# Splitting the first weight granule of five layer handovers into spare activation chunks, and giving the third granule's low part to POOL

## The reference, cut to what matters

```python
def swiglu(x, w_gate, w_up, w_down):
    return (jax.nn.silu(x @ w_gate) * (x @ w_up)) @ w_down
...
    for layer in range(DEPTH):
        f = swiglu(rmsnorm(h, nw[0]), ffn_w_gate[layer, 0], ffn_w_up[layer, 0], ffn_w_down[layer, 0])
        h = h + FFN_RES_SCALE * rmsnorm(f, nw[1])
        u = rmsnorm(h, nw[2])
        ...
        h = h + rmsnorm(m, nw[3])
        f = swiglu(rmsnorm(h, nw[4]), ffn_w_gate[layer, 1], ffn_w_up[layer, 1], ffn_w_down[layer, 1])
        h = h + FFN_RES_SCALE * rmsnorm(f, nw[5])
```

## Time and profile before

| | us |
|---|---|
| median of 3 runs | 2679.96 (2679.54 to 2680.77) |
| the profiled execution, first to last instruction | 2681.7 |
| PE busy in it | 2625.0 (98%), 12572 matmuls |
| DVE busy | 2030.9 (76%) |
| ACT busy | 1685.6 (63%) |
| POOL busy | 151.9 (6%) |
| mean granted TensorE clock | 0.992 of full speed |

### The profile page before, as it was taken

How to read it: one execution, slowest core, us unless ns; L and a number is a source line. 1 busy time by engine, 2 the same in 40 slices (tenths; PEclk the granted TensorE clock), 3 DMA queues, 4 the chain that set the end, 5 groups by cost and what they waited for, 6 DMA issues and landing times.

```text
span 2681.7 us, 35145 instructions
## 1 busy us (share of the span) xinstructions
PE 2625.0 (98%) x12572; PEld 2160.9 (81%) x12572; DVE 2030.9 (76%) x2363; ACT 1685.6 (63%) x2199; POOL 151.9 (6%) x196
## 2 busy tenths in 40 slices
PE   9999999999999999999999999999999999999998
PEld 7888788888888878888677888788887878888886
DVE  5557667777757765564668776799999999999998
ACT  5446654454457775453554444678788787878786
POOL 2000000000000001004210000200000000000020
PEclk9999999999999999999999999899999999999999
DMA  8555227768754338643148874699999999999996
GB/s 308 188 164 182 78 85 269 251 225 301 239 169 152 125 116 310 232 160 126 48 144 304 311 271 144 253 366 378 369 386 359 388 360 377 372 377 374 365 383 246
DMA packets 284589, 687.43 MB, mean 256 GB/s; under 512 B 13476, under 2 KB 22208, under 8 KB 284480
## 3 DMA queue, kind: packets, MB, share of 16 engines
q1 hardware_dynamic: 266208, 618.65, 64.5%
q0 software_dynamic: 18272, 67.32, 7.0%
HBM read 670.19 MB, written 15.73 MB: 256 GB/s over the span
## 4 chain that ended last, share of the span: by engine, by line
PE 86%; DVE 7%; ACT 5%; issue 2%; DVEq 0%; ACTq 0%; POOL 0%
PE ps L2561 26%; PE ps L2563 26%; PE ps L2562 25%; DVE w_lo L1636 2%; PE ps L2722 2%; ACT w_hi L876 2%; PE ps L2806 1%; DVE xt L2406 1%; DVE xn L1715 1%; DVE h L1720 1%; PE ps L3195 0%; DVE act_lo L1704 0%; ACT hp L1298 0%; PE ps L3261 0%; PE ps L2781 0%
## 5 line engine op out<-in xcount | busy, mean ns | idle before, releaser
L1636 DVE TENSOR_TENSOR w_lo<-w_raw,w_hi 128x1024 fp32r<-128x1024 f32 x1156 | 1396.0, 1226 | 423.0 <-ACT w_hi L876 392.7
L876 ACT ACTIVATE w_hi<-w_raw 128x1024 fp32r<-128x1024 f32 x1158 | 1214.0, 1059 | 754.8 <-PE ps L2563 752.3
L2561 PE MATMUL ps<-w_hi,act_hi 128*128 128x512 f32 (+1 forms) x3424 | 1343.1, 392 | 26.6 <-DVE w_lo L1636 17.5
L2563 PE MATMUL ps<-w_lo,act_hi 128*128 128x512 f32 (+1 forms) x3424 | 1321.0, 386 | 0.0
L2562 PE MATMUL ps<-w_hi,act_lo 128*128 128x512 f32 (+1 forms) x3424 | 1319.2, 385 | 0.0
L2561 PEld LDWEIGHTS ps<-w_hi,act_hi 128*128 128x128 f32 x3424 | 645.2, 188 | 171.7 <-DVE w_lo L1636 28.7
L2563 PEld LDWEIGHTS ps<-w_lo,act_hi 128*128 128x128 f32 x3424 | 645.0, 188 | 131.1
L2562 PEld LDWEIGHTS ps<-w_hi,act_lo 128*128 128x128 f32 x3424 | 645.9, 189 | 123.1 <-issue 1.4
L1627 DVE SCALAR_TENSOR_TENSOR scr<-scr,small 128x1024 f32<-128x1024 f32 x98 | 125.4, 1279 | 0.1
L1038 ACT ACTIVATE act_hi<-ps 128x512 fp32r<-128x512 f32 (+1 forms) x87 | 62.6, 720 | 71.9 <-PE ps L2722 71.9
L1762 DVE TENSOR_TENSOR act_lo<-ps,act_hi 128x512 fp32r<-128x512 f32 (+1 forms) x87 | 74.1, 851 | 39.7 <-ACT act_hi L1038 39.7
(11 more groups left out here) (516 smaller groups left out, 1424.0 us busy)
## 6 DMA issues: line engine op xcount, KB each, us to landing
w_raw<-in_moe_w SPq DMA_DIRECT2D x337, 1024.0 KB, 6.9
scr<-in_ada_w POOLq DMA_DIRECT2D x48, 1024.0 KB, 6.5
w_raw<-in_ffn_w_up SPq DMA_DIRECT2D x44, 1024.0 KB, 5.5
w_raw<-in_ffn_w_down SPq DMA_DIRECT2D x44, 1024.0 KB, 5.0
w_raw<-in_ffn_w_gate SPq DMA_DIRECT2D x43, 1024.0 KB, 5.3
w_raw<-in_ff_w SPq DMA_DIRECT2D x42, 1024.0 KB, 5.4
w_raw<-in_odd_w_in SPq DMA_DIRECT2D x20, 1024.0 KB, 5.0
w_raw<-in_even_w_in SPq DMA_DIRECT2D x14, 1024.0 KB, 5.3
```

Of the source, the lines that this page charges most:

```text
L876: act.activation(w_hi[:, g % SPLITS, 0:c * width], w_raw[:, s % RING, o:o + c * width], ACT.Copy).then_inc(hi_done, 1)
L1636: dve.tensor_tensor(w_lo[:, g % SPLITS, 0:c * width], w_raw[:, s % RING, o:o + c * width], w_hi[:, g % SPLITS, 0:c * width].bitcast(F32), ...
L2561: pe.matmul(out_ap, hi, whi, start=start, stop=False)
L2563: return pe.matmul(out_ap, hi, wlo, start=False, stop=stop)
```

## The change

The five handovers are marked while the slots are planned (`lead_here`, at the first granule of the next part). For each marked g0:

- its high part is written by ACT into two pairs of `act_hi` chunks (8, 9 and 14, 15) that the tail does not use, and its low part by DVE into the same chunks of `act_lo`. It waits for `gran_used` of g0 - 4 alone, and stands ahead of `post_sums(0)` and `add_post(0)`;
- the granules behind it shift by one in `w_hi` and `w_lo` (`split_at`), and wait for an older granule (`split_freed`);
- POOL makes the low part of g2 (`lo_beside`), DVE skips it;
- both transpose groups of block 0 come after the third tail granule, `h_split(0, 1)` comes ahead of `post_sums(1)` and `add_post(1)`;
- PE runs g0, g1 and g2 ahead of the transposes of block 1, keeps the 3 idle products and drops the 6.

```diff
+        def split_at(g):
+            return (g - sum(lead < g for lead in leads)) % SPLITS
+        def split_freed(g):
+            return g - SPLITS - any(g - SPLITS <= lead < g for lead in leads)
+        def apart(x):
+            return x[:].rearrange("p (a b) n -> p a (b n)", b=2)[:, 4:8:3, :]
+        def on_pool(g):
+            return g - 2 in leads
...
+            def lo_beside(i):
+                g = leads[i] + 2
+                s = g // 2
+                c, width, o = granule(s, g % 2)
+                pool.wait_ge(hi_done, g + 1)
+                pool.tensor_tensor(w_lo[:, split_at(g), 0:c * width], w_raw[:, s % RING, o:o + c * width],
+                                   w_hi[:, split_at(g), 0:c * width].bitcast(F32), ALU.subtract).then_inc(pool_lo, 1)
...
+            lo_beside(0)
+            lo_beside(1)
             pool.wait_ge(hh_done, n(hh_done, 8))
             modulation(0)
+            lo_beside(3)
+            lo_beside(4)
...
+                    if g in leads:
+                        act.wait_ge(gran_used, g - 4)
+                        act.activation(apart(act_hi), w_raw[:, s % RING, o:o + GRAN].rearrange("p (c n) -> p c n", c=2),
+                                       ACT.Copy).then_inc(hi_done, 1)
+                        continue
                     if g >= SPLITS:
-                        act.wait_ge(gran_used, n.gran(g - SPLITS + 1))
+                        act.wait_ge(gran_used, n.gran(split_freed(g) + 1))
...
             def boundary(col, late):
                 tail_end[0] = gp[0]
+                hi(1)
                 act.activation(epsc[:, 1:2], epsc[:, 0:1], ACT.Sqrt)
                 post_sums(0)
                 hi(2)
                 h_split(0, 0, col, 6)
+                h_split(0, 1, col, late)
                 post_sums(1)
-                h_split(0, 1, col, late)
-                hi(2)
+                hi(1)
                 h_split(1, 0, col, 6)
...
             def boundary(factor, col, late):
+                lo(1)
                 dve.wait_ge(wbc_in, n(wbc_in, 16))
                 add_post(0, factor)
                 lo(1)
                 h_split(0, 0, col, 6)
+                gp[0] += 1
+                h_split(0, 1, col, late)
+                add_post(1, factor)
                 lo(1)
-                add_post(1, factor)
-                h_split(0, 1, col, late)
-                lo(2)
                 h_split(1, 0, col, 6)
...
-                        if tb == 0 and k == 1:
+                        if tb == 0 and k == (1 if first else 2):
                             if first:
                                 pe.wait_ge(boot_rest, 32)
-                            if not first:
+                            else:
                                 idle_products(bank + 1, 3)
                             h_transposes(1, 0, 6, first)
                             h_transposes(1, 1, 2, first)
-                            if not first:
-                                idle_products(bank + 1, 6)
...
-                        if tb and k >= 2 and free is not None:
-                            h_transposes(0, k - 2, free if k == 3 else 6)
+                        if tb and k == 2 and free is not None:
+                            h_transposes(0, 0, 6)
+                            h_transposes(0, 1, free)
```

More of the change, by code:

```diff
@@ L382, in build_block_kernel, with lead_here @@
         slots = []
+        leads = []
+        def lead_here():
+            leads.append(2 * len(slots))
+        def split_at(g):
[6 more added lines that the diff above has]
+            return g - 2 in leads
         def plan_up(w, n0, width, split=True):
@@ L397, in steps, with granule @@
             return [(f, min(BANK, ff - f)) for f in range(0, ff, BANK)]
+        def granule(s, j):
+            _, chunks, width, _ = slots[s]
+            return chunks // 2, width, j * (chunks // 2) * width
         def plan_ff(wg, wu, wd, ff):
@@ L562, in build_block_kernel @@
         post_row(0, 3, hh_done, 4)
+        lead_here()
         for j in EV_ORDER:
@@ L680, in modulation @@
                     n(ada_sum, 4 if l == 0 and j < 8 else 2)
+                    if l == 0 and j == SUMMED_FIRST:
+                        lo_beside(2)
                     if j + 2 < 24:
@@ L1635, in lo @@
                     dve.wait_ge(hi_done, n.gran(g + 1))
-                    dve.tensor_tensor(w_lo[:, g % SPLITS, 0:c * width], w_raw[:, s % RING, o:o + c * width],
-                                      w_hi[:, g % SPLITS, 0:c * width].bitcast(F32), ALU.subtract).then_inc(lo_done, 1)
+                    if g in leads:
+                        dve.tensor_tensor(apart(act_lo), w_raw[:, s % RING, o:o + GRAN].rearrange("p (c n) -> p c n", c=2),
+                                          apart(act_hi).bitcast(F32), ALU.subtract).then_inc(lo_done, 1)
+                        continue
+                    dve.tensor_tensor(w_lo[:, split_at(g), 0:c * width], w_raw[:, s % RING, o:o + c * width],
+                                      w_hi[:, split_at(g), 0:c * width].bitcast(F32), ALU.subtract).then_inc(lo_done, 2 if on_pool(g - 1) else 1)
                     if layer[0] is not None and at_sum[0] < (48 if layer[0] else 64):
@@ L2555, in _, with low_parts @@
             gp = [0]
+            def low_parts(g):
+                if on_pool(g):
+                    pe.wait_ge(pool_lo, 1 + leads.index(g - 2))
+                else:
+                    pe.wait_ge(lo_done, n.gran(g + 1))
             def three(out_ap, chunk, cols, g, o, width, start, stop):
                 hi, lo = act_hi[:, chunk, cols], act_lo[:, chunk, cols]
-                whi, wlo = w_hi[:, g % SPLITS, o:o + width], w_lo[:, g % SPLITS, o:o + width]
+                if g in leads:
+                    whi, wlo = apart(act_hi)[:, o // BANK, :], apart(act_lo)[:, o // BANK, :]
+                else:
+                    whi, wlo = w_hi[:, split_at(g), o:o + width], w_lo[:, split_at(g), o:o + width]
                 pe.matmul(out_ap, hi, whi, start=start, stop=False)
```

27 lines of the change are left out of this document (16 added, 11 removed).

## The result

| | before | after |
|---|---|---|
| median, us | 2680.36 (2679.54 to 2680.84, 4 runs) | 2693.87 (2692.54 to 2696.83, 4 runs) |
| span of the profiled execution, us | 2681.7 | 2694.9 |
| mean granted clock | 0.992 | 0.991 |

The ratio is 1.0051, with a 95% interval of 1.0039 to 1.0063: 13.5 us slower, where 8 were forecast, and 0.4 us above the upper end of the range. First the line of the page that answers to the earlier trace rows: PE does 30 matmuls fewer and yet the span is longer.

What follows compares the result with a forecast made beforehand. PE, busy 98% of the span, was taken to bound the kernel. The new order alone would gain 2.3 us; with POOL's hold on DVE, 8 us are lost: 2689.7 against 2681.7 profiled, as median 2688 us, range 2676.5 to 2693.5.

Steps and rivals of the forecast that it cites:

- the removed products: Six idle products and the wait behind them, 1.75 us a handover, 8.8 us in all if nothing else bound.
- The rival by which they come back as time: At the handovers, the removed products become a gain of up to 8.8 us, giving 2671 us; chance 0.16.
- g4's chain: Block 1's split, sums of squares and Silu table load on ACT, then g4's high and low part; PE waits 1.3 us.
- The early split costs nothing: Splitting g0 early fits idle time on ACT (1.06 us of work) and DVE (1.23 us) ahead of block 0's sums.
- g4 ready at T + 9.15 us: At each handover g4's low part is ready 9.15 us after T, the start of the transposes of block 1.
- POOL goes in ahead of DVE's queued low part: POOL's subtraction for g2 runs between DVE's second addition to `h` and its low part of g1.
- The hold: Time POOL's subtraction keeps DVE's low part of g1 standing: 2.3 us, bounds 1.14 and 2.6.
- the gap before g0: PE stands before g0 of block 0, waiting for DVE's `act_lo` pieces: 2.05 us at each handover.
- the order's loss: PE starts g4 later than before: 1.6 us lost a handover, 8 us in all.
- chance of three or more 0.12: Rival: PE's clock falls to half behind the gap before g0, 1.7 us each, 8.5 at all five; chance 0.12.
- a gap of this size goes either way: Earlier gaps on PE: 1.94 us near 610 with grant 0.76, 1.97 us near 1639 with full grant.
- break-even: Hold of DVE's low part of g1 at which a handover neither gains nor loses: 0.72 us.

Runs made afterwards that it cites:

- E3: The kernel before without the 6 idle products behind the transposes of block 1, nothing else; 2680.46 us, ratio 0.9998.
- E1: The changed kernel, but POOL starts each subtraction only after DVE has finished the low part of g1; 2678.29 us, ratio 0.9991.
- E5: E1 plus g4's high and low part moved ahead of the sums of squares and the table load; 2673.01 us, ratio 0.9970.
- E7: The changed kernel with POOL's subtraction written as two instructions of 512 columns instead of one of 1024; 2686.06 us, ratio 1.0020.
- E4: The changed kernel with 8 idle products on PE in the gap before g0 of block 0; 2690.46 us, ratio 1.0036.
- E8: The changed kernel, collision kept, with g4's high and low part ahead of the sums of squares and table load; 2683.70 us, ratio 1.0011.
- E12: E8 with 8 idle products put into the gap before g0; 2680.71 us, ratio 1.0001, three of ten executions at 2683.79, 2685.33 and 2687.25.
- E10: The kernel before with g4's high and low part moved ahead of the sums of squares and table load, nothing else; 2685.73 us, ratio 1.0020.
- E6: The kernel before with only POOL making the low part of g2, orders, buffers and idle products unchanged; 2694.00 us, ratio 1.0048.

## Why the prediction was off

**What bounds the kernel, and the removed products: right.** E3 shows what they were worth, nothing by themselves. The rival by which they come back as time needed g4's chain not to bind, and the gap before g4 was there at all five.

**The early split costs nothing: right.** E1 has it, and its profile shows no gap between the tail and g3.

**g4 ready at T + 9.15 us: right.** Measured: 9.06 to 9.17 from T to PE's start of g4 (9.25 forecast with the restart). Taking the sums and the table load out of the way ahead of it is worth 5.3 us (E5 against E1).

**POOL goes in ahead of DVE's queued low part: right**, at all five handovers, though it asked only 0.4 us ahead of DVE's turn. The hold was 2.19 us for 2.3 forecast, the gap before g0 1.89 for 2.05, and the order's loss 1.5 us a handover for 1.6: 7.4 for 8 us. POOL's own time without the collision is 2.41 us, a little under twice the row of 512. The Trainium skill (SBUF — State Buffer, "SBUF: two separate sides") lets the one that starts first keep the shared port for its whole instruction; E7 agrees, the stand is one instruction of POOL's at a time, here 0.2 us less than the 2.41 that POOL takes alone.

**The step that failed: the clock was left out of the sum.** The prediction put it at nothing in the sum and called it a rival, "chance of three or more 0.12", with the sentence "a gap of this size goes either way". If it goes either way, a gap of about 2 us at five handovers makes two or three falls the expectation, some 4 us, and three or more is no 12% case. It fell at three of five, at 1.5 us each for 1.7 forecast. E4 shows that standing brings it on: with the gap filled there is no fall, and the time is 3.4 us less by the medians. Nothing here tells at which of the five it falls: with like gaps it was the second, third and fifth in the changed kernel, and the second, third and fourth in E8. Its term was there with its row and its price; what I did not do is multiply it by its own chance and add it. With it the sum is 7.4 + 4.5 = 11.9 of the 13.2 us between the spans. The upper end of the range did hold three falls, at 1.7 us each; that the time came out above even that, by 0.4 us, is the surplus outside the handovers, for which the prediction had no term.

**A slip that changes nothing.** The range begins at "2683 (hold 1.5)". By the prediction's own break-even a hold of 1.5 us costs (1.5 - 0.72) x 5 = 3.9 us, so it is 2684.

**What stays open:** 1.3 us of the difference between the spans, the like surplus in E4 and E7, and the three high executions of E12. The two traces show where the 1.3 us arise. From g4 of the fifth handover to the eight transposes of `h` that come next (1672.15 before, 1688.08 after) the changed kernel takes 3.1 us longer, and behind them 2.7 us less; 0.7 of the rest lie between the first and the second handover. The clock moved with it. Windows of the kernel before, at 1391 and 1639, and of the changed kernel at the same places of the program, at 1404 and 1653:

```profile
1391.00:1398.00 7.00, 6.88 (x31) 5.24 (x30) 5.87 (x10) 5.76 (x10) 2.18 (x3) 1.00 0.63 207
1639.00:1646.00 7.00, 6.99 (x36) 5.62 (x37) 2.64 (x4) 3.37 (x8) 0.00 (x0) 1.00 0.46 152
...
1404.00:1411.00 7.00, 6.96 (x26) 5.40 (x25) 5.21 (x9) 4.72 (x9) 2.18 (x3) 0.76 0.64 216
1653.00:1660.00 7.00, 6.76 (x20) 4.52 (x21) 2.72 (x4) 2.13 (x6) 0.00 (x0) 0.76 0.46 159
```

Each stands behind a gap on PE that both kernels have (2.72 and 2.74 us; 1.97 us), and the change does not touch these places. In all, TensorE ran at half clock for 40.3 us before, and for 40.8 us outside the handovers after: not more of it, but in other places. So the 1.3 us look like the balance of falls that moved, and not like work of the change; no run tests that.

## What to carry to other kernels

Before work is given to POOL to relieve DVE, read in DVE's timeline what it does in SBUF just then, and who waits for it; let POOL start behind that instruction (one wait, worth 15.6 us here by the medians), or cut its work into pieces, which leaves half of the stand (E7). When rows say that an effect goes either way at a place that comes five times, its mean belongs into the sum. A buffer that comes free early is worth something only if the instruction that fills it is moved forward as well, and moving it without the buffer costs time (E5 and E10).

## What the hardware showed

- Five like gaps of 1.89 or 1.90 us, and the clock fell behind three of them; behind E6's 2.06 to 2.08 us it fell at two of five. It fell behind none of E3's gaps of 1.51 us or E7's of 0.79. Idle products in the gap kept it up (E4). The gap of 1.97 us of the earlier trace rows, at 1639 in the kernel before, stands in all fourteen traces at 1.97 or 1.98 us, and the clock fell behind it in five of them: the same gap at the same place goes either way from one execution to the next. The Trainium skill (TensorE: Matmul & The Clock Gate, "What's actually happening") has the gate close after a whole idle window. Read as the prediction read it, that allows no fall behind gaps of this size; three of the five gaps of 1.89 us brought one, and the measurement decides.
- DVE and POOL took turns by single instructions at every handover, and the one that asked while the other worked was next: POOL between two of DVE's in the changed kernel (2.19 us) and E6 (2.17 us), DVE between two of POOL's in E7 (1.09 us).
- `SCALAR_TENSOR_TENSOR` with two SBUF operands (`xn`, `h`) was held as `TENSOR_TENSOR` was (E6, 2.17 us); with its tensor operand in PSUM and `act_hi` in SBUF it was not (E1, 2.15 us for eight, beside POOL).
